# Query-subkey scores from scaled fp16 pairs, with eight smaller moves of work in a two-layer encoder kernel

## The chip, the core and the metric

The kernel is one program on one core of a Trainium2 chip. A core has TensorE (PE in the profile, its weight loads are PEld), VectorE (DVE), ScalarE (ACT), GpSimd (POOL) and SyncE (SP, which here issues nearly all DMAs). Each engine runs its own instruction list in order, and the lists meet only at semaphores. The time is device microseconds of one execution; lower is better.

## The reference, cut to what matters

Two layers run one after the other on x, which is 256 tokens x 1024 channels in float32. Each layer mixes tokens (2-D neighbourhood attention and a long convolution, merged by gates, one output projection, added to x). Then comes the expert retrieval, of which this part matters here:

```python
h = rmsnorm(x, norm2_g[l])
q = (h @ wq).reshape(C, PEER_HEADS, 2, half)             # 8 heads, 2 sides, half = 128
s = jnp.einsum('thpd,hpkd->thpk', q, subkeys)            # 128 subkeys a side
sv, si = lax.top_k(s, PEER_TOPK)                         # 16 best of each side
...
u = u_tab[eid]; a = gelu(einsum('tc,thkc->thk', h, u))   # 128 x 128 experts in all
out = einsum('thk,thkc->tc', g * a, v_tab[eid])
```

## The kernel before, in words

**Weights come as a stream.** All matrices lie in HBM as tiles of 128x1024 float32. SP loads them one after the other into a ring of 4 slots (`refill`). ACT makes of each a scaled fp16 tile `w_hi` (L545) and, for most, scales the float32 tile in place (L552); then POOL (L494) or DVE (L937) subtracts to get the fp16 rest `w_lo`. Activations are held in the same way as a high and a low fp16 part. A product of two matrices is then three fp16 products: high by high, high by low, low by high. `contract` (L1603 to L1617) is one such tile: 16 matmuls of L1611 and 8 of L1615, 256 columns each.

**Stages of a layer.** Tiles 0 to 39 project the input for attention, convolution and gates, 40 to 47 are the two up-projections, 48 to 55 the output projection (`T_OUT`), 56 to 71 the sixteen query tiles (`T_WQ`), 72 to 199 the expert table `u` (`T_U`), 200 to 327 the table `v`.

**The query stage, around which the prediction turns.** Query tile n (0 to 15, two of them for a head) is accumulated in PSUM bank n % 4, from `raw_hi[2]` and `raw_lo[2]`, the residual rows not yet divided by their root mean square. DVE reads the bank, multiplies by the inverse root mean square and writes float32 queries into SBUF: `scale_queries(w, s)` for tile 4w+s (L1389 to L1401), which signals `q2_ready`. PE starts tile n only when `q2_ready` says that tile n-4 has left the bank (L1993). In the same lists, DVE and ACT also make the normalised rows for the expert stage: `make_h` (L998) writes a pair of rows to PSUM, ACT's `norm_high` (L648) copies the pair as fp16, `h_low` (L1006) subtracts. `normalised(2, between)` (L1010) writes out this order by hand and calls `between(s)` at four places in it; with s it scales query tile 4+s. ACT's list for tiles 4 to 7 is: split the next ring tile (`split_behind`, L545 and L552, which waits until PE has finished the tile four before), then `norm_high`.

**Scores.** `subk` holds the layer's subkeys in float32, loaded by a DMA of 1 MB that ACT issues (L817). 32 matmuls a layer of 128x128 by 128 columns, native float32, make the scores in banks 4 to 7 (L2004). ACT copies each bank out (L832, `score_copied`), and DVE searches the top 16 (L1408 on). The first four groups of scores wait for 4, 8, 12 and 16 queries, the last four for a copied bank.

**The rest of the order that the change touches.** `layer_loads` (L398) is SP's list of small loads between the ring's refills. `MASK_AFTER` (L77) says behind which weight tile POOL adds the attention mask to which head's bias. The start of a layer's DVE list (L1092 to L1107), ACT's list around the first normalisation (L685 to L714), around the first softmax heads (L763 to L787), in the up-projection (L800) and in the output projection (L811 to L815), and PE's list between attention and the up-projection (L1900 to L1902) are all written out by hand.

## Time and profile before

| | us |
|---|---|
| median of 3 runs | 1885.17 (1878.71 to 1885.3) |
| the profiled execution's own time | 1882.93 |
| its span, first to last instruction | 1880.9 |
| PE busy | 1861.9 (99%) |
| ACT busy | 1320.0 (70%) |
| DVE busy | 1198.5 (64%) |
| POOL busy | 965.4 (51%) |
| DMA queue of the ring and tables | 58.5% of 16 engines |

The shares are means over the stages. A matmul's end is modelled, so its recorded time (273 ns for 256 columns) is longer than the distance to the next one (about 109 ns) and a short wait of PE can hide in it. The granted clock of TensorE is 1.0 at 2.4 GHz and 0.5 at 1.2 GHz; its mean is 0.998.

### The profile page before, as it was taken

The page shows a single profiled execution, that of the slowest core. Times are in us where ns is not written, and L with a number is a line of the kernel's source. Part 1 is how long each engine was busy: PE and PEld are TensorE (multiplying, and loading weights), DVE is VectorE, ACT ScalarE, POOL GpSimd, SP SyncE. Part 2 cuts the span into 40 slices and gives each one's busy share as a digit, 9 for nine tenths or more (in the row PEclk, how much of TensorE's full clock was granted, in tenths as well). Part 3 has the DMA queues.
Part 4 walks back from the last instruction along what each step waited for, and adds up shares of the span by engine and source line. Part 5 has one row for each costly group of instructions (what it writes and reads, how often), then busy time and mean ns, then how long its engine had stood idle before and what let it go on. Part 6 is the DMA issues. An engine that isn't in the chain of part 4 may idle for free.

```text
span 1880.9 us, 42913 instructions
## 1 busy us (share of the span) xinstructions
PE 1861.9 (99%) x14238; PEld 1352.6 (72%) x14238; DVE 1198.5 (64%) x2529; ACT 1320.0 (70%) x1885; POOL 965.4 (51%) x636
## 2 busy tenths in 40 slices
PE   9899999999999999999999999999999999999999
PEld 7788898899999444444467888988999984444444
DVE  7857489677776444444487573996777764444444
ACT  7877988887777555555578788889877765555554
POOL 1746868876666222222217468687767752222221
PEclk9999999999999999999999999999999999999999
DMA  8644656564555666666575446565555556666664
GB/s 286 177 151 148 228 169 201 201 191 167 167 178 175 204 202 202 203 203 205 191 234 178 157 155 225 169 201 190 191 178 168 168 187 202 203 202 203 204 203 136
DMA packets 100325, 357.39 MB, mean 190 GB/s; under 512 B 11744, under 2 KB 13730, under 8 KB 99492
## 3 DMA queue, kind: packets, MB, share of 16 engines
q1 hardware_dynamic: 99828, 354.36, 58.5%
q10 hardware_dynamic: 432, 2.18, 0.3%
q8 instruction: 39, 0.64, 0.1%
q14 instruction: 26, 0.21, 0.0%
HBM read 355.45 MB, written 1.05 MB: 190 GB/s over the span
## 4 chain that ended last, share of the span: by engine, by line
PE 89%; DVE 4%; ACT 4%; DMA 1%; issue 1%; SPq 0%; ACTq 0%; DVEq 0%
PE bank L2085 35%; PE bank L1611 31%; PE bank L1615 15%; PE bank L2024 3%; ACT w_hi L545 1%; ACT ring L552 1%; DMA ring<-stream 1%; PE bank L2004 1%; DVE w_lo L937 1%; PE bank L1827 0%; ACT raw_hi L604 0%; PE bank L1910 0%; PE bank L1859 0%; DVE bank L998 0%; DMA xT<-x_in 0%
## 5 line engine op out<-in xcount | busy, mean ns | idle before, releaser
L494 POOL TENSOR_TENSOR w_lo<-ring,w_hi 128x1024 f16<-128x1024 f32 x360 | 770.6, 2142 | 413.1 <-ACT ring L552 412.8
L545 ACT ACTIVATE w_hi<-ring 128x1024 f16<-128x1024 f32 x654 | 684.4, 1047 | 33.4 <-PE bank L1597 13.1
L1611 PE MATMUL bank<-act_parts,w_hi 128*128 128x256 f16 x4992 | 597.8, 273 | 0.1
L937 DVE SCALAR_TENSOR_TENSOR w_lo<-ring,w_hi 128x1024 f16<-128x1024 f32 x294 | 361.2, 1229 | 349.0 <-ACT w_hi L545 348.9
L1611 PEld LDWEIGHTS bank<-act_parts,w_hi 128*128 128x128 f16 x4992 | 486.0, 98 | 64.2 <-issue 5.9
L517 POOL TENSOR_TENSOR e_lo<-arena,e_hi 128x256 f16<-128x256 f16 x256 | 174.5, 683 | 482.6 <-ACT e_hi L851 482.6
L2085 PE MATMUL bank<-w_hi,e_hi 128*128 128x512 f16 x1024 | 388.1, 379 | 0.0
L2085 PE MATMUL bank<-w_lo,e_hi 128*128 128x512 f16 x1024 | 388.1, 379 | 0.0
L2085 PE MATMUL bank<-w_hi,e_lo 128*128 128x512 f16 x1024 | 388.1, 379 | 0.0
L552 ACT ACTIVATE ring<-ring 128x1024 f32<-128x1024 f32 x360 | 377.3, 1048 | 0.0
L1615 PE MATMUL bank<-act_parts,w_lo 128*128 128x256 f16 x2496 | 324.2, 273 | 0.0
L851 ACT ACTIVATE e_hi<-arena 128x256 f16 (+1 forms) x256 | 105.9, 416 | 304.8 <-PE bank L2085 304.8
L1615 PEld LDWEIGHTS bank<-act_parts,w_lo 128*128 128x128 f16 x2496 | 244.6, 98 | 28.8
L2085 PEld LDWEIGHTS bank<-w_hi,e_lo 128*128 128x128 f16 x1024 | 100.2, 98 | 120.8
L2085 PEld LDWEIGHTS bank<-w_lo,e_hi 128*128 128x128 f16 x1024 | 100.2, 98 | 120.4
L2085 PEld LDWEIGHTS bank<-w_hi,e_hi 128*128 128x128 f16 x1024 | 100.2, 98 | 120.4
L860 ACT ACTIVATE bank<-bank 128x256 f32<-128x256 f32 x136 | 50.0, 368 | 108.4 <-PE bank L1615 102.3
L1527 DVE SCALAR_TENSOR_TENSOR arena<-arena,bank 128x512 f32 (+1 forms) x128 | 79.4, 682 | 70.8 <-PE bank L2024 70.8
L1516 DVE TENSOR_TENSOR weighted_j<-onehot_j,bank 128x512 f16<-128x512 f16 x256 | 94.8, 411 | 0.0
L1535 DVE TENSOR_TENSOR arena<-arena,bank 128x256 f32 (+1 forms) x136 | 56.8, 418 | 34.1 <-ACT bank L860 24.4
L1611 PE MATMUL bank<-raw_hi,w_hi 128*128 128x256 f16 x336 | 75.6, 273 | 0.8 <-DVE xT L1107 0.8
L1611 PE MATMUL bank<-raw_lo,w_hi 128*128 128x256 f16 x336 | 75.6, 273 | 0.0
(265 smaller groups left out, 1679.8 us busy)
## 6 DMA issues: line engine op xcount, KB each, us to landing
ring<-stream SPq DMA_DIRECT2D x654, 512.0 KB, 4.1
arena<-rpb_in SPq DMA_DIRECT2D x8, 512.0 KB, 8.0
arena<-subkeys ACTq DMA_DIRECT2D x2, 1024.0 KB, 7.7
ring<-stream SPq DMA_DIRECT2D x4, 256.0 KB, 5.0
xT<-x_in SPq DMA_DIRECT2D x4, 256.0 KB, 5.1
arena<-w_in SPq DMA_DIRECT2D x2, 512.0 KB
arena<-decay_in SPq DMA_DIRECT2D x2, 512.0 KB
arena<-dft_in SPq DMA_DIRECT2D x2, 512.0 KB, 5.2
```

Source lines behind the costliest of these rows:

```text
L494: pool.tensor_tensor(w_lo[:, slot, :], ring[:, slot, :], w_hi[:, slot, :], ALU.subtract).then_inc(low_by_pool.sem, 1)
L517: pool.tensor_tensor(e_lo[:, n % RING, :], experts[:, bass.ds(i * RING + n, 1), :].rearrange("p a t -> p (a t)"), e_hi[:, n % RING, :], AL ...
L545: nc.scalar.activation(w_hi[:, slot, :], ring[:, slot, :], ACT.Copy, scale=TABLE_SCALE).then_inc(hi_ready.sem, 1)
L552: nc.scalar.activation(ring[:, slot, :], ring[:, slot, :], ACT.Copy, scale=TABLE_SCALE).then_inc(ring_scaled.sem, 1)
L851: nc.scalar.activation(e_hi[:, n % RING, :], experts[:, bass.ds(i * RING + n, 1), :].rearrange("p a t -> p (a t)"), ACT.Copy).then_inc(e_h ...
L937: V.scalar_tensor_tensor(w_lo[:, slot, :], ring[:, slot, :], TABLE_SCALE, w_hi[:, slot, :], ALU.mult, ALU.subtract).then_inc(low_by_vector ...
L1516: ins = V.tensor_tensor(weighted_j[:, n % BURST, a, :, :, :], onehot_j[:, a, :, :].unsqueeze(1).to_broadcast(wide), pair_weights(a).unsque ...
L1527: V.scalar_tensor_tensor(w, w, EXPERT_SCALE / WEIGHT_SCALE, bank[ROUTE_BANKS[n]][:, :].rearrange("p (t j) -> p j t", t=TOK), ALU.mult, ALU ...
L1535: V.tensor_tensor(w, w, source[n % 2], ALU.mult).then_inc(late_stored.sem, 1)
L1611: T.matmul(out_, weights(w_hi, tile, k), moving[:, k, :], start=(k == 0 and moving is hi), stop=False, skip_group_check=True)
L1615: ins = T.matmul(out_, weights(w_lo, tile, k), hi[:, k, :], start=False, stop=(k == KT - 1), skip_group_check=True)
L2085: ins = T.matmul(bank[4 + 2 * half + tt][:, :], e_[:, slot, tokens], w_[:, slot, columns], start=first and w_ is w_hi and e_ is e_hi, stop ...
```

## The change

The queries are no longer kept in float32. DVE scales the bank in place (`q2_scaled`), ACT copies it as fp16 (`query_high`, `q2_hi_ready`), and DVE subtracts (`query_low`), which is now what signals `q2_ready`. The subkeys are split once a layer, by one ACT and one DVE instruction of 128x2048. The scores become three fp16 products each. Beside that, work is moved: SP's small loads come later and the transform table `dft` in two halves; POOL's mask additions come later; ACT's `norm_high` of the first normalisation comes one tile later each; the first heads' exponentials and normalisation come ahead of a convolution step and a weight split; the second half of the mixed spectrum and its copy come earlier; the last attention part comes later; at the end of the output projection two weight splits come behind the last rows; at the start of the second layer a weight split and a copy change places.

```diff
-MASK_AFTER = (16, 17, 19, 21, 25, 27, 29, 31)
+MASK_AFTER = (21, 22, 23, 25, 27, 29, 31, 33)
...
-        q2T = part(24, 2 * PH, S)
+        q2_hi, q2_lo = halves("q2_hi", 24, 2 * PH), halves("q2_lo", 32, 2 * PH)
+        sub_hi, sub_lo = (halves(name, kb)[:, :, :].rearrange("p k (a n) -> p (k a) n", a=2)
+                          for name, kb in (("sub_hi", 48), ("sub_lo", 52)))
...
                 for slot in range(RING):
                     refill(l, 0, 1, slot)
-                    taps(slot)
                 for slot in range(RING):
                     refill(l, 0, 2, slot)
                     if slot == 0:
-                        small(table_in, dft, dft_in)
+                        small(taps_in, spread, spread_in)
                     elif slot == 2:
-                        small(tables_in, mask, mask_in)
...
+                for slot in range(RING):
+                    refill(l, 0, 3, slot)
+                    if slot == 1:
+                        small(taps_in, skip[0:1, :], skip_in[at, :])
+                        small(taps_in, decay[:, :, :], decay_in)
+                    elif slot == 3:
+                        small(table_in, dft[:, 0:2, :, :], dft_in[:, 0:2, :, :])
...
-                    if 4 <= m <= 6:
-                        norm_high(1, ((0,), (1, 2), (3,))[m - 4])
+                    if m >= 5:
+                        norm_high(1, (m - 5,))
...
+                head_exp(0)
                 hyena_in(10)
-                head_exp(0)
+                head_exp(1)
                 hyena_in(11)
-                head_exp(1)
...
                     raw_high(2, m, bank[4 + m % 4][:, 0:S])
                     square_one(m)
-                    split_behind(T_OUT + m)
+                    if m < KT - 2:
+                        split_behind(T_OUT + m)
+                split_behind(T_OUT + KT - 2)
+                split_behind(T_OUT + KT - 1)
...
+                def query_high(n):
+                    act.wait_ge(q2_scaled.sem, q2_scaled.at(l, n + 1))
+                    nc.scalar.activation(q2_hi[:, n, :], bank[n % 4][:, 0:S], ACT.Copy).then_inc(q2_hi_ready.sem, 1)
                 for s in range(RING):
                     split_behind(T_WQ + s)
                 for s in range(RING):
+                    query_high(s)
                     split_behind(T_WQ + RING + s)
                     norm_high(2, (s,))
-                for tile in range(T_WQ + 3 * RING, T_U + RING):
-                    high_part(l, 0, tile)
-                    scale_tile(tile)
+                for n in range(RING, 2 * PH):
+                    query_high(n)
+                    if n == RING:
+                        act.wait_ge(subk_in.sem, subk_in.at(l, 16))
+                        nc.scalar.activation(sub_hi, subk[:, :, :], ACT.Copy, scale=TABLE_SCALE
+                                             ).then_inc(sub_hi_ready.sem, 1)
+                    if n >= 2 * RING:
+                        high_part(l, 0, T_WQ + RING + n)
+                        scale_tile(T_WQ + RING + n)
...
                 def scale_queries(w, s):
                     dve.wait_ge(tile_done.sem, tile_done.at(l, w * RING + (T_WQ + s + 1)))
-                    V.tensor_tensor(q2T[:, bass.ds(w * RING + s, 1), :].rearrange("p a t -> p (a t)"),
-                                    bank[s % 4][:, 0:S], norm_tmp[:, 2, :], ALU.mult).then_inc(q2_ready.sem, 1)
+                    V.scalar_tensor_tensor(bank[s % 4][:, 0:S], bank[s % 4][:, 0:S], 1.0 / TABLE_SCALE,
+                                           norm_tmp[:, 2, :], ALU.mult, ALU.mult).then_inc(q2_scaled.sem, 1)
+                def query_low(w, s):
+                    dve.wait_ge(q2_hi_ready.sem, q2_hi_ready.at(l, w * RING + s + 1))
+                    n = bass.ds(w * RING + s, 1)
+                    V.tensor_tensor(q2_lo[:, n, :].rearrange("p a t -> p (a t)"), bank[s % 4][:, 0:S],
+                                    q2_hi[:, n, :].rearrange("p a t -> p (a t)"), ALU.subtract
+                                    ).then_inc(q2_ready.sem, 1)
                 for s in range(RING):
                     scale_queries(0, s)
                 dve.wait_ge(out_used.sem, out_used.at(l, 8))
-                normalised(2, lambda s: scale_queries(1, s))
-                with dve.Fori(2, (T_U - T_WQ) // RING) as w:
+                def second_queries(s):
+                    query_low(0, s)
+                    scale_queries(1, s)
+                normalised(2, second_queries)
+                dve.wait_ge(sub_hi_ready.sem, sub_hi_ready.at(l, 1))
+                V.scalar_tensor_tensor(sub_lo, subk[:, :, :], TABLE_SCALE, sub_hi, ALU.mult, ALU.subtract
+                                       ).then_inc(sub_ready.sem, 1)
+                with dve.Fori(1, (T_U - T_WQ) // RING - 1) as w:
                     for s in range(RING):
-                        scale_queries(w, s)
+                        query_low(w, s)
+                        scale_queries(w + 1, s)
+                for s in range(RING):
+                    query_low(3, s)
...
-                pe.wait_ge(subk_in.sem, subk_in.at(l, 16))
+                pe.wait_ge(sub_ready.sem, sub_ready.at(l, 1))
...
-                        ins = T.matmul(bank[4 + g][:, c * P:(c + 1) * P], q2T[:, m, tt * P:(tt + 1) * P],
-                                       subk[:, m, :], start=True, stop=True)
+                        tokens, rows = slice(tt * P, (tt + 1) * P), bank[4 + g][:, c * P:(c + 1) * P]
+                        T.matmul(rows, q2_hi[:, m, tokens], sub_hi[:, m, :], start=True, stop=False)
+                        T.matmul(rows, q2_hi[:, m, tokens], sub_lo[:, m, :], start=False, stop=False)
+                        ins = T.matmul(rows, q2_lo[:, m, tokens], sub_hi[:, m, :], start=False, stop=True)
```

PE's condition for query tile n is the same line as before, `pe.wait_ge(q2_ready.sem, q2_ready.at(l, w * RING + (s - 3)))`; what counts up `q2_ready` is another instruction now.

DVE's list of the kernel before, in each layer from the first normalised rows of the query stage (L998 is `make_h`, L1392 scales a query tile, L1006 is `h_low`):

```order
L998 SCALAR_TENSOR_TENSOR bank<-xT,cols_sb,bank 128x256 [waits out_used]
L998 SCALAR_TENSOR_TENSOR bank<-xT,cols_sb,bank 128x256 x3
L1392 TENSOR_TENSOR arena<-bank,norm_tmp 128x256 [waits tile_done]
L1006 TENSOR_TENSOR act_parts<-bank,act_parts 128x512 [waits h_hi_ready]
L998 SCALAR_TENSOR_TENSOR bank<-xT,cols_sb,bank 128x256 [waits h_ready]
L998 SCALAR_TENSOR_TENSOR bank<-xT,cols_sb,bank 128x256
L1392 TENSOR_TENSOR arena<-bank,norm_tmp 128x256 [waits tile_done]
```

The same stretch of DVE's list in the changed kernel (L1026 is `make_h`, L1430 `query_low`, L1423 the scaling, L1034 `h_low`):

```order
L1026 SCALAR_TENSOR_TENSOR bank<-xT,cols_sb,bank 128x256 [waits out_used]
L1026 SCALAR_TENSOR_TENSOR bank<-xT,cols_sb,bank 128x256 x3
L1430 TENSOR_TENSOR q_lo<-bank,q_hi 128x256 [waits q2_hi_ready]
L1423 SCALAR_TENSOR_TENSOR bank<-bank,norm_tmp 128x256 [waits tile_done]
L1034 TENSOR_TENSOR act_parts<-bank,act_parts 128x512 [waits h_hi_ready]
L1026 SCALAR_TENSOR_TENSOR bank<-xT,cols_sb,bank 128x256 [waits h_ready]
L1026 SCALAR_TENSOR_TENSOR bank<-xT,cols_sb,bank 128x256
L1430 TENSOR_TENSOR q_lo<-bank,q_hi 128x256 [waits q2_hi_ready]
L1423 SCALAR_TENSOR_TENSOR bank<-bank,norm_tmp 128x256 [waits tile_done]
```

The subtraction for query tile 0 now stands behind all four `make_h` instructions, and the one for tile 1 behind the scaling of tile 4, `h_low` and two more `make_h` instructions.

ACT's list of the changed kernel in the same stage, from the fourth split of the stage to the split of the subkeys (L553 and L560 are a ring tile's split, L840 is `query_high`, L656 `norm_high`, L852 `sub_hi`; of the four rounds of L840, L553, L560, L656 the list has between them, the first and the beginning of the next stand here as one run):

```order
L553 ACTIVATE w_hi<-ring 128x1024 [waits tile_done,ring_full3]
L560 ACTIVATE ring<-ring 128x1024
L840 ACTIVATE q_hi<-bank 128x256 [waits q2_scaled]
L553 ACTIVATE w_hi<-ring 128x1024 [waits tile_done,ring_full0]
L560 ACTIVATE ring<-ring 128x1024
L656 ACTIVATE act_parts<-bank 128x512 [waits h_made]
L840 ACTIVATE q_hi<-bank 128x256 [waits q2_scaled]
```

In the kernel before this list reads the same without L840, so the first query's fp16 copy now stands behind four whole splits.

## Rows read from the trace of the kernel before

**Rows 1.** Busy time of each engine (the page).
```profile
PE 1861.9 (99%) x14238; PEld 1352.6 (72%) x14238; DVE 1198.5 (64%) x2529; ACT 1320.0 (70%) x1885; POOL 965.4 (51%) x636
```

**Rows 2.** Waits of PE: line waited for, us in total, times, longest.
```profile
PE bank L1787 <- ACT arena L707: 3.5, 1, 3.5
PE bank L1976 <- DVE raw_lo L971: 2.5, 2, 1.2
PE bank L1859 <- DVE arena L1215: 2.4, 2, 1.2
PE bank L1910 <- DVE arena L1290: 1.5, 2, 0.7
PE bank L1611 <- DVE xT L1107: 0.8, 1, 0.8
```

**Rows 3.** The chain in order of time: start, us, what; scores, routing.
```profile
238.27 7.15 PE bank L2004 x64
...
408.51 1.84 PE bank L2024 x32
```

**Rows 4.** ACT in order of time, end of output projection: start, us, instruction.
```profile
194.09 0.40 ACT L635 ACTIVATE bank<-bank 128x256 f32<-128x256 f32 x1
...
207.89 1.04 ACT L552 ACTIVATE ring<-ring 128x1024 f32<-128x1024 f32 x1
```

**Rows 5.** DVE in order of time, the same stretch and on to query tile 4.
```profile
195.58 0.43 DVE L1379 SCALAR_TENSOR_TENSOR bank<-bank,xT 128x256 f32<-128x256 f32 x1
...
206.87 0.42 DVE L1392 TENSOR_TENSOR arena<-bank,norm_tmp 128x256 f32<-128x256 f32 x1 [1.27 <-PE bank L1615]
207.21 1.66 DVE L998 SCALAR_TENSOR_TENSOR bank<-xT,cols_sb,bank 128x256 f32<-128x256 f32 x4
```

**Rows 6.** PE in order of time, last rows of query tile 4, first of 5.
```profile
208.41 1.04 PE L1615 MATMUL bank<-raw_hi,w_lo 128*128 128x256 f16 x8
209.29 0.27 PE L1611 MATMUL bank<-raw_hi,w_hi 128*128 128x256 f16 x1
```

**Rows 7.** ACT in order of time behind query tile 4.
```profile
209.55 1.06 ACT L545 ACTIVATE w_hi<-ring 128x1024 f16<-128x1024 f32 x1 [0.62 <-PE bank L1615]
...
211.46 0.58 ACT L648 ACTIVATE act_parts<-bank 128x512 f16<-128x512 f32 x1
```

**Rows 8.** DVE in order of time behind query tile 4, and scaling query 9.
```profile
212.07 0.69 DVE L1006 TENSOR_TENSOR act_parts<-bank,act_parts 128x512 f16<-128x512 f32 x1 [2.16 <-ACT act_parts L648]
212.79 0.88 DVE L998 SCALAR_TENSOR_TENSOR bank<-xT,cols_sb,bank 128x256 f32<-128x256 f32 x2
213.58 0.42 DVE L1392 TENSOR_TENSOR arena<-bank,norm_tmp 128x256 f32<-128x256 f32 x1
...
222.73 0.42 DVE L1392 TENSOR_TENSOR arena<-bank,norm_tmp 128x256 f32 x1 [1.78 <-PE bank L1615]
```

**Rows 9.** Groups by line: busy us, mean ns of one.
```profile
L545 ACT ACTIVATE w_hi<-ring 128x1024 f16<-128x1024 f32 x654 | 684.4, 1047 | 33.4 <-PE bank L1597 13.1 <-PE bank L1615 8.6 <-DMA ring<-stream 8.0
L937 DVE SCALAR_TENSOR_TENSOR w_lo<-ring,w_hi 128x1024 f16<-128x1024 f32 x294 | 361.2, 1229 | 349.0 <-ACT w_hi L545 348.9
```

**Rows 10.** Windows: from:to, length, busy us of PE, PEld, DVE, ACT, POOL, PEclk, DMA share, GB/s.
```profile
50.00:52.00 2.00, 0.33 (x4) 0.32 (x4) 2.00 (x2) 1.99 (x3) 2.00 (x1) 0.59 0.99 246
52.00:54.00 2.00, 2.00 (x13) 1.22 (x10) 1.93 (x5) 2.00 (x5) 0.11 (x1) 0.50 1.11 317
...
58.00:60.00 2.00, 2.00 (x26) 1.52 (x19) 1.44 (x3) 2.00 (x4) 0.47 (x1) 1.00 0.87 270
...
190.00:200.00 10.00, 8.61 (x75) 7.15 (x73) 4.76 (x13) 9.98 (x15) 8.33 (x5) 1.00 0.71 247
```

**Rows 11.** The chain: a tile's 16 high matmuls there and later; the table's load.
```profile
39.69 8.20 DMA ring<-stream
...
52.37 3.53 PE bank L1611 x16
...
261.13 1.75 PE bank L1611 x16
```

More of the change, by code:

```diff
@@ L431, in layer_loads @@
                     if slot == 0:
-                        small(table_in, dft, dft_in)
+                        small(taps_in, spread, spread_in)
                     elif slot == 2:
-                        small(tables_in, mask, mask_in)
-                for r in range(ROWS):
-                    for slot in (2 * (r % 2), 2 * (r % 2) + 1):
-                        refill(l, 0, 3 + r // 2, slot)
-                        if slot % 2 == 0:
-                            offsets(r)
-                for group in range(5, T_UP // RING + 1):
+                        small(taps_in, w3, w3_in[at].rearrange("a p b n -> (a p) b n"))
+                for slot in range(RING):
[5 more added lines that the diff above has]
+                        small(table_in, dft[:, 0:2, :, :], dft_in[:, 0:2, :, :])
+                for group in (4, 5):
                     for slot in range(RING):
                         refill(l, 0, group, slot)
+                        if slot % 2:
+                            offsets(2 * (group - 4) + slot // 2)
+                        elif group == 4 and slot == 0:
+                            small(tables_in, mask, mask_in)
+                for group in range(6, T_UP // RING + 1):
+                    for slot in range(RING):
+                        refill(l, 0, group, slot)
+                        if group == 7 and slot == 0:
+                            small(back_in, dft[:, 2:4, :, :], dft_in[:, 2:4, :, :])
                 with sp.Fori(0, (T_VT - T_UP) // RING) as i:
@@ L710, in act_layer @@
                 split_behind(T_V)
+                norm_high(1, (3,))
                 split_behind(T_V + 1)
@@ L739, in act_layer, with gate @@
                     hyena_in(n)
-                def gate(m):
+                def gate(m, between=None):
                     tile_wait(T_GATE + m)
@@ L745, in gate @@
                                          bias=half_gate_b[:, l, m:m + 1]).then_inc(tile_copied.sem, 1)
+                    if between is not None:
+                        between()
                     split_behind(T_GATE + m)
@@ L776, in act_layer @@
                         head_exp(h + 1)
-                    gate(2 * h + 1)
+                    gate(2 * h + 1, (lambda: keep_even(1)) if h == NH - 1 else None)
                     if h % 2 and h + 2 < NH:
@@ L800, in act_layer @@
                 for n in range(T_UP, T_OUT - 1):
+                    if n == T_UP + 4:
+                        merged_high(0)
+                        merged_high(1)
                     split_behind(n)
@@ L1095, in dve_layer @@
                             add_delta(b, delta[b][:, :])
+                    if l and b0:
+                        low_part(l, 0, HEAD)
                     for b in (b0, b0 + 1):
@@ L1105, in dve_layer @@
                         low_part(l, 0, HEAD + b // 2)
-                    if l:
-                        V.tensor_copy(x_pair(b), delta[b][:, :]).then_inc(x_kept.sem, 1)
+                    elif l and b == 0:
+                        low_part(l, 0, HEAD + 1)
                 dve.wait_ge(sq_used.sem, sq_used.at(l, KT // 2))
@@ L1295, in dve_layer @@
                 real_products(1)
-                attention_parts(NH // 2 - 1)
                 def up_product(m):
@@ L1881, in pe_layer, with up @@
                         turn_mixed()
-                def up(n, wait=None):
+                def up(n):
                     for j in (0, 1):
@@ L1892, in up @@
                         for k in range(4):
-                            if wait is not None:
-                                wait(k)
                             first, parts = (0, (attn_hi, attn_lo)) if n < 4 else (4, (act_hi, act_lo))
@@ L1898, in up @@
                         ins.then_inc((up_half, tile_done)[j].sem, 1)
-                mixed_spectrum(1, 0)
-                mixed_spectrum(1, 1)
-                up(0, lambda k: pe.wait_ge(attn_ready.sem, attn_ready.at(l, k + 1)))
+                pe.wait_ge(tile_copied.sem, tile_copied.at(l, 36))
+                parts_ready(0, T_UP)
+                for ks in (range(3), (3,)):
+                    for j in (0, 1):
+                        for k in ks:
+                            pe.wait_ge(attn_ready.sem, attn_ready.at(l, k + 1))
+                            ins = product(bank[j][:, 0:S], T_UP, 4 * j + k, k, k == 0, k == 3, (attn_hi, attn_lo))
+                        if k == 3:
+                            ins.then_inc((up_half, tile_done)[j].sem, 1)
                 up(1)
```

34 lines of the change are left out of this document (18 added, 16 removed).

## The prediction

> **What bounds the kernel now.** I read the busy line first: PE is busy 99% of the span, 1861.9 us, no other engine more than 70% [rows 1]. So an edit counts if it changes PE's work or makes PE wait; the other engines' time is free until PE waits for it. Next the waits of PE [rows 2]: 3.5 us once for the sine of the filter network, then pairs of 1.2, 1.2 and 0.7, one per layer, and 0.8 at the second layer's start. These five rows are 10.7 us, smaller ones some 3 more, so there is little to win by reordering, and much to lose. Third the chain, for what the scores cost: one layer's 32 float32 products stand as 64 matmul records in 7.15 us [rows 3]. Last, the query stage on all three engines, for that is where the change puts new steps between PE and the bank that it wants.
>
> **A tile and its end.** A query tile is 24 matmuls and takes 2.62 us (16 of them 1.75 [rows 11], the other 8 start 0.88 before the next tile [rows 6]). I call T the moment at which PE would start the next tile; for query tile 4 it is 209.29 [rows 6]. ACT's next split, waiting for that tile's end, starts at T+0.26 [rows 7]; a DVE scaling that waits for tile 9 starts at 222.73, where T is 222.39 (209.29 and five tiles), so at T+0.34 [rows 8].
>
> **The scores.** The changed kernel has 96 fp16 matmuls a layer, 128 columns each. The nearest row has the same shape and type: 32 of them in 1.84 us, 57.4 ns each [rows 3], hence 5.5 us against 7.15. ACT's copies are behind them, though: ACT has the last query's copy (0.4) and a split (1.9) ahead of the first bank copy, so the fifth group of scores waits about 0.8. The gain is 1.65 - 0.8, about 0.8 a layer, 1.6 in all. The Trainium skill speaks against the rows here: "TensorE: Matmul & The Clock Gate", section on the back-to-back issue gap, gives about 81 ns for a matmul of 128 columns in a stream with weight loads. By it 96 of them would be 7.8 us, an estimate from that page, and the scores 0.6 us a layer slower than float32; the sum would be some 4.6 us higher. The routing rows, which load weights for every matmul too, show 57.4, so I go by them.
>
> **The query stage, step by step.** `q2_ready` is what lets PE reuse a bank. Before, one DVE instruction behind the tile's end gave it, 3 tiles ahead of need. Now it comes from `query_low`, and that stands in DVE's list behind work that itself waits for later tiles.
>
> Tile 4 wants the low part of query 0. Its fp16 copy stands in ACT's list behind the root and four splits. Before, the last of these ends at 208.93 [rows 4]. The two splits moved behind the output rows don't delay those rows, but ACT idles for the last of them: its square ends at 194.49 [rows 4] and DVE makes the last row at 195.58+0.43 [rows 5], so root and splits come 1.6 later and end at 210.5. Copy 0.4 and subtraction 0.4 give 211.3. PE would be ready at 206.67, or 0.2 earlier, since the last row saves PE that much of its 1.2 wait. The stall is 4.8. Without the 1.6 it would be 3.1; DVE's own list alone (206.87, then 207.21+1.66 [rows 5], then 0.4) would still give 2.6.
>
> Tile 5 wants the low part of query 1. Ahead of it on DVE stands `h_low`, which waits for ACT's `norm_high`, which stands behind a split that waits for tile 4. The trace has this run: split at T+0.26, `norm_high` at T+2.17 to T+2.75 [rows 7], `h_low` at T+2.78, two `make_h` at T+3.50, and free at T+4.29 [rows 8]. Plus 0.42 for the subtraction (the scaling's duration; same operands and size) and 0.06 to PE: 4.8. Before, nobody waited for this run. Tile 6 has the same run behind tile 5: 4.8. Tile 7 has it without `make_h`: 3.9.
>
> Tile 8 wants the low part of query 4, behind the last `h_low` and the subkeys' split. ACT: `norm_high` done as above, one copy to T+3.0, then `sub_hi`, 2048 elements. From 1047 ns for 1024 and 0.58 for 512 I get 2.0 [rows 7, 9]: T+5.0. DVE: `sub_lo` twice the 1229 ns of 1024 less its fixed part, 2.25 [rows 9]: T+7.3. Then the loop's entry and the subtraction: T+7.8. All of it is a stall: 7.8.
>
> Tiles 9 to 15: `query_low(w, s+1)` stands behind `scale_queries(w+1, s)`, which waits for the tile that PE has just finished. So each tile starts after T+0.34, 0.36 for the scaling, 0.45 for the subtraction, 0.06: 1.2 each, 8.4 for seven.
>
> Sum per layer: 4.8 + 4.8 + 4.8 + 3.9 + 7.8 + 8.4 = 34.5, twice 69.0. As bounds I take 57 (3.1 for tile 4, 6.5 for tile 8, 0.9 for each of the seven) and 75 (1.6 for each of the seven, since registers and separate wait instructions lie between them, which no row shows).
>
> **What the stalls do to TensorE's clock.** The trace has one idle of 3.5 us, ahead of the sine's product at 51.7 [rows 2]. The granted clock is 0.59 on the mean from 50 to 52, 0.5 (1.2 GHz) from 52 to 54 and back at 1.0 from 58 [rows 10]. The 16 high matmuls right behind it take 3.53 us instead of 1.75 [rows 11], so a tile at the low level costs 2.6 more. Five stalls a layer are longer than that idle (4.8, 4.8, 4.8, 3.9, 7.8), so I charge the tile behind each: 5 x 2.6 = 13 a layer, 26 in all. From below it is 0 (the clock holds); from above the stage never gets back, as short stalls go on to its end: 12 tiles x 2.6 and 5.5 of scores, 37 a layer.
>
> **The other moves.** The idle of 3.5 ends with a chain through a ring tile that took 8.2 us to land [rows 11]; the change puts about 0.5 MB less of tables in front of it and 1.1 MB later still. If that idle goes, so does its half clock, about 2.9: 6.4 together, of which I take 5. The pairs of 1.2 (softmax against a convolution step), 0.7 (spectrum) and the 0.8 of layer two [rows 2] each have their edit, 4.6 together; I take 4. Nothing new waits there: what moves back has its consumer later in PE's list. So -9, with 0 and -12 as ends. ACT and POOL gain time in the stalls, which PE's later tiles don't need: they are behind PE nowhere else in [rows 2].
>
> **The sum**, against the profiled execution's own 1882.9 (2.0 above its span, 2.2 below the median 1885.2): 1882.9 + 69.0 + 26 - 1.6 - 9 = 1967.3. I predict 1967.
>
> **Rivals.**
> The clock holds, or falls only in the longest stall. For it: the wait of 1.2 before the last output row's products left it at 1.0 [rows 10]. Against it: [rows 10]. The time is 1882.9 + 69 - 1.6 - 9 = 1941, with one fall a layer 1947.
> The clock stays at the low level through tiles 9 to 15 and the scores. For it: those tiles go in bursts with stalls of 1.2. Against it: at [rows 10] it was back within some 6 us of steady work. The time is 1941 + 74 = 2015, with half of the seven 1990.
> Not slower: the new signal comes in time. This would need the subtractions to run before PE asks, so that scores and moves alone are left: 1882.9 - 3.3 - 9 = 1871. It decides at a mean stall of 12.3/24, 0.5 us for each of the 24 tiles from 4 on. Against it stands the order of DVE's list, which makes at least T+0.34 plus two instructions unavoidable for every tile from 9, and [rows 7, 8] for 5 to 7.
> The reordered loads and lists miss their aim (the sine still waits, as its tile is still gated by the same subtraction): 1967 + 9 = 1976. For it: a ring tile is only reloaded after its low part. It lies inside the range.
>
> **How the numbers follow.** Forecast as summed 0.60, clock holds 0.17, clock stays low 0.13, moves without gain 0.07, not slower 0.03. The likeliest case's own range is 1950 to 1985. The range that should hold 8 in 10 reaches down to 1938, to take in the held clock with fewer us of stall, and up to 2000. A measurement of this kernel can't tell less than 0.5%, 9.4 us, from no change; all cases but one lie far above 1895. So slower 0.97, same 0.01, faster 0.02.
>
> **What would show it.** PE waits for the DVE line of `query_low`, some 12 a layer, together near 34 us; at tiles 4 to 8 single idles of 4 to 8 us, the longest behind `sub_lo`; idles near 1.2 from there. A granted clock of 0.5 between about 211 and 250 us in layer one, and the same in layer two. Scores at 57 ns a matmul. The sine's wait below 2 us. It is wrong if PE's waits in the query stage stay below 10 us a layer, or if the stage from the last output tile to the scores' end grows by less than 30 us.

## The result and the profile after

The changed kernel takes 1970.45 us (median of 3 runs, 1968.0 to 1971.21) against 1885.17 before: a ratio of 1.0462, 95% interval 1.0442 to 1.0482. The forecast was 1967. Its profiled execution has a span of 1968.4 us against 1880.9, so 87.5 us are to be placed.

The busy line of the page, against [rows 1]:

```profile
PE 1883.8 (96%) x14302; PEld 1358.2 (69%) x14302; DVE 1223.8 (62%) x2563; ACT 1332.0 (68%) x1919; POOL 969.6 (49%) x636
```

PE has 22 us more of busy time (its matmuls at the low clock count as longer) and 66 us more of idle time; its mean granted clock is 0.982 (before 0.998). The waits of PE (line waited for, us in total, times, longest), against [rows 2]:

```profile
PE bank L1662 <- DVE q_lo L1430: 64.0, 24, 7.4
PE bank L1878 <- DVE arena L1229: 3.3, 2, 3.2
PE bank L1910 <- DVE arena L1246: 2.7, 2, 2.0
PE bank L1644 <- DVE act_parts L1353: 2.3, 2, 1.1
PE bank L2035 <- DVE raw_lo L999: 2.0, 2, 1.0
PE bank L2064 <- ACT arena L860: 1.3, 2, 0.6
...
PE bank L1838 <- ACT arena L715: 0.4, 1, 0.4
```

One row is new and holds nearly everything: 24 waits for the subtraction of `query_low`, twelve a layer, as forecast. The sine's 3.5 is down to 0.4 (last row), but 3.3 at L1878 and 2.3 at L1644 are where 0.5 or less stood. They come back below.

Where the stage lies in the span, PE in order of time: the mean-square product that opens the query stage, and the first product of the expert table behind the scores. Before:

```profile
198.27 0.70 PE L1647 MATMUL bank<-norm_tmp,mats 128*128 128x256 f32 x2 [0.15 <-DVE norm_tmp L982]
...
245.25 0.93 PE L1611 MATMUL bank<-act_parts,w_hi 128*128 128x256 f16 x7
```

After, with the first matmul of query tiles 4 to 10 and the last three scores between them (the bracket is PE's idle time just before, and what ended it):

```profile
196.49 0.70 PE L1698 MATMUL bank<-norm_tmp,mats 128*128 128x256 f32 x2 [0.15 <-DVE norm_tmp L1010]
...
210.34 0.39 PE L1662 MATMUL bank<-raw_hi,w_hi 128*128 128x256 f16 x1 [5.29 <-DVE q_lo L1430]
220.29 0.39 PE L1662 MATMUL bank<-raw_hi,w_hi 128*128 128x256 f16 x1 [4.68 <-DVE q_lo L1430]
230.27 0.39 PE L1662 MATMUL bank<-raw_hi,w_hi 128*128 128x256 f16 x1 [4.68 <-DVE q_lo L1430]
239.34 0.39 PE L1662 MATMUL bank<-raw_hi,w_hi 128*128 128x256 f16 x1 [3.77 <-DVE q_lo L1430]
251.23 0.39 PE L1662 MATMUL bank<-raw_hi,w_hi 128*128 128x256 f16 x1 [7.45 <-DVE q_lo L1430]
257.45 0.28 PE L1662 MATMUL bank<-raw_hi,w_hi 128*128 128x256 f16 x1 [0.92 <-DVE q_lo L1430]
261.17 0.28 PE L1662 MATMUL bank<-raw_hi,w_hi 128*128 128x256 f16 x1 [0.92 <-DVE q_lo L1430]
...
288.56 0.22 PE L2064 MATMUL bank<-sub_hi,q_hi 128*128 128x128 f16 x1
288.62 0.22 PE L2065 MATMUL bank<-sub_lo,q_hi 128*128 128x128 f16 x1
288.67 0.22 PE L2066 MATMUL bank<-sub_hi,q_lo 128*128 128x128 f16 x1
288.73 1.91 PE L1662 MATMUL bank<-act_parts,w_hi 128*128 128x256 f16 x16
```

The stretch grows from 46.98 to 92.24 us in layer 1, and from 46.98 to 89.53 in layer 2: 87.8 of the 87.5 us. Everything else in the kernel sums to about nothing. I use this stretch as the yardstick below, because nearly all the waits that vary with the loads lie outside it.

Two numbers come out of these rows. From 257.45 to 261.17 are 3.72 us, 1.10 more than a tile's 2.62, where the record says 0.92 of idle: about 0.17 of each wait hides behind the last matmul's modelled end. And the distance between starts, less the next idle, is what a tile took: tile 4 took 220.29 - 4.68 - 210.34 = 5.27, tile 9 took 2.80. So tiles 4 to 8 of layer 1 cost 2.5, 2.5, 2.5, 1.7 and 2.5 more than at the full clock, in layer 2 1.6, 2.2, 2.5, 1.4 and 2.4. The windows beside them (columns as in [rows 10]):

```profile
208.00:210.00 2.00, 0.00 (x0) 0.00 (x0) 0.23 (x1) 1.74 (x3) 2.00 (x2) 0.66 0.40 107
210.00:212.00 2.00, 1.66 (x8) 1.19 (x9) 0.20 (x1) 0.00 (x0) 2.00 (x1) 0.50 0.77 242
212.00:214.00 2.00, 2.00 (x12) 1.42 (x10) 0.00 (x0) 0.00 (x0) 0.06 (x1) 0.50 0.84 283
...
216.00:218.00 2.00, 0.00 (x0) 0.00 (x0) 0.08 (x1) 2.00 (x3) 0.21 (x1) 1.00 0.00 0
218.00:220.00 2.00, 0.00 (x0) 0.00 (x0) 1.74 (x4) 0.47 (x2) 1.91 (x1) 0.72 0.00 0
```

The granted clock (the third number from the right, 1.00 until 208) falls while PE stands idle, from 208 to 210, is 0.5 over tile 4, is back at 1.0 when PE stands idle again at 216, and falls anew before 220. Part of the low level thus lies over time in which PE does nothing, and costs nothing there.

The stall of tile 8 in full, against [rows 7, 8] (ACT, then DVE):

```profile
243.88 1.06 ACT L553 ACTIVATE w_hi<-ring 128x1024 f16<-128x1024 f32 x1 [5.45 <-PE bank L1666]
244.84 1.04 ACT L560 ACTIVATE ring<-ring 128x1024 f32<-128x1024 f32 x1
245.79 0.58 ACT L656 ACTIVATE act_parts<-bank 128x512 f16<-128x512 f32 x1
246.27 0.37 ACT L840 ACTIVATE q_hi<-bank 128x256 f16<-128x256 f32 x1
246.53 1.91 ACT L852 ACTIVATE sub_hi<-arena 128x2048 f16<-128x2048 f32 x1
```
```profile
243.82 0.43 DVE L1423 SCALAR_TENSOR_TENSOR bank<-bank,norm_tmp 128x256 f32<-128x256 f32 x1 [4.62 <-PE bank L1666]
246.40 0.69 DVE L1034 TENSOR_TENSOR act_parts<-bank,act_parts 128x512 f16<-128x512 f32 x1 [2.14 <-ACT act_parts L656]
248.47 2.29 DVE L1445 SCALAR_TENSOR_TENSOR sub_lo<-arena,sub_hi 128x2048 f16<-128x2048 f32 x1 [1.38 <-ACT sub_hi L852]
250.68 0.42 DVE L1430 TENSOR_TENSOR q_lo<-bank,q_hi 128x256 f32 x1
```

PE's tile ends near 243.7. Then one step follows another: ACT's split of a ring tile, its copies of the rows and of a query, `sub_hi`, and on DVE `sub_lo` and the subtraction. PE starts at 251.23. `sub_lo` takes 2.29 where 2.25 was worked out, `sub_hi` 1.91 for 2.0.

### The profile page after: what moved, and what is told of

Read it like the earlier page. It is cut to its first block, busy times and chain, and to the rows that moved or that the text cites. A ratio compares the mean times of both kernels' runs of the same rounds, so it can differ in the third digit from the quotient of the medians.

```text
span 1968.4 us, 43125 instructions
## 1 busy us (share of the span) xinstructions
PE 1883.8 (96%) x14302; PEld 1358.2 (69%) x14302; DVE 1223.8 (62%) x2563; ACT 1332.0 (68%) x1919; POOL 969.6 (49%) x636
## 4 chain that ended last, share of the span: by engine, by line
PE 82%; DVE 6%; ACT 6%; DMA 3%; issue 2%; POOL 1%; SPq 0%; DVEq 0%; ACTq 0%
PE bank L2146 34%; PE bank L1662 28%; PE bank L1666 14%; PE bank L2085 3%; DMA ring<-stream 2%; ACT w_hi L553 2%; ACT ring L560 2%; DVE w_lo L965 1%; POOL w_lo L502 1%; DVE bank L1026 1%; DVE q_lo L1430 0%; DMA arena<-rpb_in 0%; DVE arena L1246 0%; PE bank L1992 0%; PE bank L1969 0%
## 5 line engine op out<-in xcount | busy, mean ns | idle before, releaser
L553 ACT ACTIVATE w_hi<-ring 128x1024 f16<-128x1024 f32 x654 | 684.3, 1047 | 78.3 <-PE bank L1666 50.1
L965 DVE SCALAR_TENSOR_TENSOR w_lo<-ring,w_hi 128x1024 f16<-128x1024 f32 x294 | 372.0, 1265 | 348.6 <-ACT w_hi L553 348.5
L560 ACT ACTIVATE ring<-ring 128x1024 f32<-128x1024 f32 x360 | 377.1, 1048 | 0.0
L1662 PE MATMUL bank<-raw_hi,w_hi 128*128 128x256 f16 x336 | 91.0, 307 | 64.0 <-DVE q_lo L1430 64.0
L1662 PEld LDWEIGHTS bank<-raw_hi,w_hi 128*128 128x128 f16 x336 | 36.7, 109 | 78.8 <-issue 71.6
L1662 PE MATMUL bank<-raw_lo,w_hi 128*128 128x256 f16 x336 | 90.9, 307 | 0.0
```

Source lines behind the costliest of these rows:

```text
L553: nc.scalar.activation(w_hi[:, slot, :], ring[:, slot, :], ACT.Copy, scale=TABLE_SCALE).then_inc(hi_ready.sem, 1)
L560: nc.scalar.activation(ring[:, slot, :], ring[:, slot, :], ACT.Copy, scale=TABLE_SCALE).then_inc(ring_scaled.sem, 1)
L965: V.scalar_tensor_tensor(w_lo[:, slot, :], ring[:, slot, :], TABLE_SCALE, w_hi[:, slot, :], ALU.mult, ALU.subtract).then_inc(low_by_vector ...
L1662: T.matmul(out_, weights(w_hi, tile, k), moving[:, k, :], start=(k == 0 and moving is hi), stop=False, skip_group_check=True)
```

## The experiments

All were run beside the kernel before; its median was 1883.12 in the first set, 1881.3 in the second, 1882.23 in the third, so ratios are compared, not times. The diffs show the lines of an edit on which it turns, not the whole edit.

**The parts apart.** The first kernel has the moves alone: the changed kernel with the old queries, the old scores and `scale_queries` alone in `normalised`.

```diff
-                    query_low(0, s)
                     scale_queries(1, s)
```

> All the moves of the change, with float32 queries and scores as before. Theory: the whole loss is in the query stage. The changed kernel's trace starts the query stage's second tile 1.8 us earlier in layer one and then, from there to the same place of layer two, runs 1.3 us longer apart from the stage itself, so the moves are worth about nothing: 1885, ratio 0.998 to 1.002. Rival, the term of the prediction: the moves give 9 us, 1876, ratio 0.995.

Measured: 1884.25 us, ratio 1.0005 (0.9992 to 1.0019). The second has the pairs alone, in the kernel before:

```diff
                 for s in range(RING):
+                    query_high(s)
                     split_behind(T_WQ + RING + s)
```

> The kernel before with the fp16 pairs alone, no moves. Theory: 1971, ratio near 1.046, with the same five long and seven short waits of PE a layer. Rival: the moves of work help elsewhere by 9 us, then 1980. A second rival, that the moved splits of the output projection cause tile 4's wait: then its wait falls from 5.3 and 4.3 to about 3.1.

Measured: 1961.79 us, ratio 1.0418 (1.04 to 1.0435), and a query stage of 88.96 and 86.98 us. So the pairs are the slowdown, and the moves, for which I had booked 9 us of gain, bring none. But the pairs alone came 9 us lower than my theory had them (7 us by the ratios, 1.0462 against 1.0418): pairs and moves together are dearer than their sum. Of this kernel, the start of tiles 4 and 5 in layer 2:

```profile
1182.43 0.28 PE L1649 MATMUL bank<-raw_hi,w_hi 128*128 128x256 f16 x1 [3.15 <-DVE q_lo L1417]
1189.90 0.39 PE L1649 MATMUL bank<-raw_hi,w_hi 128*128 128x256 f16 x1 [4.68 <-DVE q_lo L1417]
```

Tile 4 waits 3.15 (2.97 in layer 1) instead of 4.3 to 5.3, and in layer 2 it then runs at full clock: 1189.90 - 4.68 - 1182.43 = 2.79. In layer 1, after 2.97, it took 4.46.

**The link between them.** Pairs, and of the moves only the two weight splits behind the last output rows:

```diff
-                    split_behind(T_OUT + m)
+                    if m < KT - 2:
+                        split_behind(T_OUT + m)
+                split_behind(T_OUT + KT - 2)
+                split_behind(T_OUT + KT - 1)
```

> The kernel before with the pairs and with one of the moves, the two weight splits of the output projection put behind the last rows. Theory A (this move is what makes the pairs dearer beside the moves): the first query's fp16 copy comes some 1.6 us later, tile 4's wait grows to 5.3 and 4.3 us in the two layers, and the clock falls at tile 4 in both layers, 1.7 to 2.6 us each; 2 x (1.6 + 1.7 to 2.6) less the last row's 0.4 gives 6 to 8 us over the 1961.8 of the pairs alone, 1968 to 1970. Theory B (the addition comes from elsewhere: the two later moves, or another clock pattern): no more than 2 us over the pairs alone, 1962 to 1964.

Measured: 1965.88 us, ratio 1.045 (1.0427 to 1.0473). Tile 4 now waits 4.32 in both layers and runs at the low clock in both; the query stage is 89.73 and 89.76, so 0.8 and 2.8 longer than with the pairs alone. The time lies between the two theories, and its interval overlaps that of the pairs alone; the rows of tile 4 decide. Theory A holds in kind, at about two thirds of its size in layer 2 and less in layer 1, where the clock had already fallen. The mechanism shows on ACT: it has nothing to do until DVE delivers the last output row, and the split that would have filled the time stands behind it (this is the same row as in the changed kernel, 194.51 there):

```profile
196.70 0.47 ACT L610 ACTIVATE raw_hi<-bank,cols_sb 128x256 f16<-128x256 f32 x1 [1.55 <-DVE bank L1400]
```

The changed kernel's tile 4 in layer 1 waits another 0.97, since one of its splits found its ring tile not landed:

```profile
203.69 1.06 ACT L553 ACTIVATE w_hi<-ring 128x1024 f16<-128x1024 f32 x1 [0.86 <-DMA ring<-stream]
```

**The clock.** The changed kernel with matmuls that only keep PE busy while it would wait, their results going to an unused bank; nothing is left out:

```diff
+                fill = {4: 17, 5: 19, 6: 19, 7: 15, 8: 31}
+                for n in range(RING, 2 * PH):
+                    for _ in range(fill.get(n, 0)):
+                        T.matmul(bank[5][:, 0:P], w_rest[:, :], w_rest[:, :], start=True, stop=True)
```

> The changed kernel, with zero float32 products of 128x128 by 128 columns into an unused bank put ahead of PE's waits for query tiles 4 to 8 (17, 19, 19, 15 and 31 of them, each about 0.22 us and together less than the wait, so that PE is busy in most of it); PE's loop over these tiles is written out. It splits wait from clock. Theory: the waits end at the same distance from the tile before, the granted clock stays at 1.0 and tiles 4 to 8 take 2.6 us: by the tile times in the trace that gives back 11.7 us in layer one and 10.0 in layer two, 1949. Rival: the slow tiles are part of the waiting (weights that come late) and not the clock: then 1970.

Measured: 1947.19 us, ratio 1.0349 (1.0329 to 1.0368). The windows of the stage are at 1.00 throughout, where the changed kernel has 0.67 or 0.68 in each ten us from 210 to 260:

```profile
210.00:220.00 10.00, 9.64 (x88) 9.13 (x87) 2.76 (x6) 4.52 (x6) 2.13 (x1) 1.00 0.39 133
...
230.00:240.00 10.00, 9.55 (x87) 9.11 (x86) 3.75 (x4) 5.38 (x8) 2.13 (x1) 1.00 0.33 105
```

The query stage is 79.70 and 78.75 us, 12.5 and 10.8 less than in the changed kernel, 23.3 in all. Not all of that is the clock. The steps of tiles 9 to 15, which were at 1.00 in both kernels and have no filling, are 3.64 instead of 3.71, and the stalls of tiles 4 to 8 are shorter by as much: 24 x 0.07 = 1.7. PE's loop over the tiles is written out in this kernel, which is the likely reason, but that was not tried by itself. What the clock took is the rest, 21.6. The waits themselves stayed nearly as long, only filled: tiles 4 and 5 start 7.40 us apart, 2.62 of tile and 4.78 of stall, where the changed kernel has 4.68 + 0.17.

**Single stalls.** Only the split of the subkeys comes three tiles later, on ACT as shown, and on DVE behind the subtraction of query 6:

```diff
-                    if n == RING:
+                    if n == RING + 3:
                         act.wait_ge(subk_in.sem, subk_in.at(l, 16))
```

> The changed kernel with one thing moved: the split of the subkeys (one ACT and one DVE instruction, 128x2048) stands three tiles later, behind the copy and the subtraction of queries 7 and 6. Theory A (tile 8's wait of 7.4 us is the run of work before it plus the split's 3.6): tile 8 waits 3.8 us, the same 3.6 us appear again as a wait only as far as the split still stands ahead of a later subtraction (tile 10 or 11 waits 2 to 4.5 instead of 0.9), time 1970 - 0 to 7, so 1963 to 1970. Theory B (the split is worth what it delays tile 8 by, and costs nothing later): 1963 or less, and no wait over 1.5 us behind tile 8.

Measured: 1961.21 us, ratio 1.042 (1.04 to 1.0441), 0.0042 or 7.9 us below the changed kernel (the two query stages are 8.2 shorter). Tile 8 waits 3.77, like tile 7, and the next waits are short:

```profile
245.35 0.39 PE L1663 MATMUL bank<-raw_hi,w_hi 128*128 128x256 f16 x1 [3.77 <-DVE q_lo L1430]
251.58 0.28 PE L1663 MATMUL bank<-raw_hi,w_hi 128*128 128x256 f16 x1 [0.93 <-DVE q_lo L1430]
```

Theory B is right: the split is worth 2 x 3.68 and comes back nowhere. Three tiles later it stands in the time in which DVE waits for PE's next tile anyway: DVE's idle time before the next scaling falls from 2.96 to 0.34.

In the next kernel the order is changed for tiles 9 to 15 alone. The subtractions of queries 5 to 7 no longer stand behind a scaling, and those of the later queries stand behind the scaling of the next query, not of the third one after:

```diff
-                with dve.Fori(1, (T_U - T_WQ) // RING - 1) as w:
+                for s in range(RING):
+                    query_low(1, s)
+                for w in (2, 3):
                     for s in range(RING):
-                        query_low(w, s)
-                        scale_queries(w + 1, s)
-                for s in range(RING):
-                    query_low(3, s)
+                        scale_queries(w, s)
+                        if w == 3 or s:
+                            query_low(w, s - 1) if s else query_low(w - 1, 3)
+                query_low(3, 3)
```

> The changed kernel with the order changed for tiles 9 to 15 alone: there the subtraction of a query stands one tile later than the scaling that frees it, so that the scaling of the tile just finished is no longer ahead of the subtraction that PE waits for. Theory A (each of these waits is only the scaling and the subtraction behind the tile's end, nothing else): the fourteen waits of about 0.9 in the records vanish, tiles 4 to 8 wait as before, 14 x 1.09 = 15.3 us less, 1955. Theory B (the copies on ACT, which stand behind its splits, take the DVE order's place as what is late): half of it or less, 1962 to 1970.

Measured: 1955.64 us, ratio 1.0389 (1.0366 to 1.0411). Its waits of PE:

```profile
PE bank L1664 <- DVE q_lo L1430: 51.8, 10, 7.5
```

Ten waits instead of 24: all fourteen short ones are gone. 0.0073 of 1882 is 13.7 us of the 15.3 expected, the rest within the intervals; the two query stages are 16.1 shorter. Theory A.

**The order turned round.** The changed kernel with every subtraction one tile behind the scaling, and the first copies between the splits on ACT:

```diff
-                    query_low(0, s)
+                    query_low(0, 3) if s == 0 else query_low(1, s - 1)
                     scale_queries(1, s)
```

> The changed kernel with another order alone: ACT copies a query's high part right behind the split that the tile's end allows (the first three behind the second split), and DVE subtracts one tile later than it scales, with the subkeys' split behind the second of the last eight tiles. Theory: tile n's low part is ready about 3 us behind its end, PE wants the bank 7.9 us behind it, so no waits are left: 1970 - 68 of waits - 22 of clock = 1880 to 1882, ratio 0.996 to 0.998. Rival: ACT, now with 0.36 a query and 1.9 for the subkeys more, falls behind PE's 2.62 us a tile and the ring's splits come late: then waits on the high parts and 1890 or more.

Measured: 1885.99 us, ratio 1.0016 (1.0004 to 1.0029), above the 1880 to 1882 of my theory. The order was the whole slowdown but for some 4 us (the stages are 48.87 and 48.80), since two waits stood where I had expected none, 2.8 in all at tile 4 and 3.8 at the scores:

```profile
PE bank L1885 <- DVE arena L1233: 4.4, 2, 2.3
PE bank L2071 <- DVE q_lo L1433: 3.8, 2, 2.0
PE bank L1669 <- DVE q_lo L1433: 2.8, 2, 1.6
```

The last query's copy stands on ACT behind a split, and the subtraction behind it. So the same order went into the kernel before, with no move at all, and that split was put behind the fourth copy of the scores (the diff is against the order just described):

```diff
                 for n in range(2 * RING, 2 * PH):
-                    high_part(l, 0, T_WQ + RING + n)
-                    scale_tile(T_WQ + RING + n)
+                    if n < 2 * PH - 1:
+                        high_part(l, 0, T_WQ + RING + n)
+                        scale_tile(T_WQ + RING + n)
                     query_high(n)
...
+                    if n == 3:
+                        high_part(l, 0, T_U + RING - 1)
+                        scale_tile(T_U + RING - 1)
```

> The kernel before with the pairs alone, the subtractions put one tile behind the scaling on DVE, the fp16 copies of the first queries put between ACT's splits, the last query's copy put ahead of the last split, and that split behind the fourth score copy. Theory A (the scores are worth 1.65 us a layer, and nothing of them is lost once no copy is late): no wait over 0.3 us for a subtraction, no wait of 2.0 before the last groups of scores; 1883.1 - 3.3 = 1879.8, a ratio of 0.997 to 0.999. Theory B (the copies on ACT and the subtractions on DVE always cost PE something at tile 4 and at the scores): 1883 to 1886, ratio 1.000 to 1.002.

Measured: 1878.52 us, ratio 0.998 (0.9965 to 0.9994): 0.2% below the kernel before, and the interval just leaves out 1. The stage shows it without scatter. In layer 2 the query stage takes 45.19 us, 1.79 less than before, with no wait for a subtraction; in layer 1 one of 1.5 at tile 4 stays, behind a split that waited 2.71 for its ring tile, so theory A holds but for that. The 16-bit products are thus a small gain, in layer 2 of the size that [rows 3] had promised.

**Where the moves' gain went.** The changed kernel once more, with the pairs in the good order, the later loads, masks, `norm_high` and the earlier spectrum kept, and four moves taken back, of which these are two:

```diff
-                    if n == T_UP + 4:
-                        merged_high(0)
-                        merged_high(1)
                     split_behind(n)
...
-                head_exp(0)
                 hyena_in(10)
-                head_exp(1)
+                head_exp(0)
                 hyena_in(11)
+                head_exp(1)
```

What the expectation calls the late last attention part is the first of them: ACT's copies of the first two merged rows, which the changed kernel has ahead of a weight split. DVE's late attention part itself stays.

> The changed kernel with the same order of copies and subtractions as in the kernel just described, with its later loads, its later masks, its later norm_high and its spectrum move kept, and with four moves taken back: the softmax heads' order, the late last attention part, the output projection's splits, and the start of the second layer. Theory A (the kept moves take the sine's idle of 3.5 and its half clock of 2.9, and the waits of the others came from the four that are taken back): 1883.1 - 3.3 - 6.4 - 1.5 = 1872, ratio 0.993 to 0.996. Theory B (the later table loads crowd ring tiles and turn the sine's idle into another wait in the first layer): one wait of 2 to 3.5 us in the first layer before the sine or behind it, 1878 to 1882, ratio 0.997 to 1.000.

Measured: 1878.62 us, ratio 0.999 (0.9977 to 1.0002). The query stage takes 45.19 and 45.20, and the sine's wait is gone, but there are waits of 2.36, 2.00 and 1.70 at two lines of attention:

```profile
PE bank L1912 <- DVE arena L1245: 3.9, 3, 2.0
...
PE bank L1880 <- DVE arena L1228: 2.4, 1, 2.4
```

Theory B in kind, though one of the waits is in layer 2. The same with the loads and masks as before (the edit is that of the last kernel below, in the same places):

> The best combination of the last call with the table loads, the transform table's halves and the masks as in the kernel before; kept are the pairs in the order without waits, the later norm_high of the first normalisation and the earlier spectrum. Theory A (the later loads bring nothing that lasts: they take away the sine's idle and give two waits of 2.0 to 2.4 on the tables): as fast as with them or faster, a ratio of 0.996 to 0.999, the waits of 2.4 and 2.0 gone, the sine's idle back at least in one layer. Theory B (they bring the 6 us forecast): slower than with them, ratio 1.000 to 1.002.

Measured: 1878.97 us, ratio 0.9977 (0.9964 to 0.999), theory A; the wait of 2.36 is gone, those of 2.0 and 1.7 are the 1.2 and 1.2 of [rows 2] again, and the sine's is back, 4.8 in layer 1 of this execution:

```profile
PE bank L1838 <- ACT arena L713: 4.8, 1, 4.8
...
PE bank L1910 <- DVE arena L1243: 2.4, 2, 1.2
```

And the moves alone with the loads and masks as before:

```diff
-MASK_AFTER = (21, 22, 23, 25, 27, 29, 31, 33)
+MASK_AFTER = (16, 17, 19, 21, 25, 27, 29, 31)
```

> The moves without the pairs, and of the moves the table loads, the transform table's halves and the mask additions put back as in the kernel before. Theory A (the later loads take the sine's idle, but cost about as much by a later wait with half clock in the first layer): the sine's idle of 3.5 is back with its half clock, the wait of some 3 us behind it is gone, and the time is that of all the moves together, 1884 within 1.5. Theory B (the loads gain the 6.4 us that I forecast, and the order moves lose as much): 1888 to 1891. Theory C (the loads cost more than they gain): 1879 to 1882.

Measured: 1884.05 us beside 1881.3, ratio 1.0016 (1.0001 to 1.0031), against 1.0005 with the later loads. The sine waits 1.3 and 2.4 us. Of the three, theory A is the nearest: the loads trade one wait for others, and no pair of kernels with and without them can be told apart. The intervals (some 2.5 us each way) leave a gain or loss of 2 us open.

## Why the forecast came near: two sizes off, in opposite directions

Taken step by step against the changed kernel's profile:

- **Order of the subtractions, 69.0 us forecast.** The records give 64.0 in 24 waits, and 24 x 0.17 hidden behind modelled ends: 68.1. By tile in layer 1 (forecast, record + 0.17): 4.8, 5.5; 4.8, 4.85; 4.8, 4.85; 3.9, 3.9; 7.8, 7.6; and 1.2, 1.1 for each of the seven. The reading of [rows 7, 8], a run of dependent instructions that nobody waited for until a new wait was put behind it, is what carried the forecast; the two kernels under Single stalls confirm two of its terms by taking them away. The lower bound of this term was added up wrongly: the terms that the prediction names give 2 x 29.4 = 59, not 57. Nothing hangs on it.
- **Tile 4.** Forecast 3.1 without the 1.6 of ACT's idle time at the last output row, and 4.8 with it. The runs show 3.1 and 3.3 in the pairs alone, 4.5 with the splits moved (0.17 added). The step held, and it is a case of an edit that looks harmless, a split moved behind rows that it would not have delayed, and that costs only because a new consumer stands at the end of the same list.
- **The clock, 26 us forecast.** The tiles cost 11.7 and 9.9, in sum 21.6; the filled kernel, from the other side, gives the same, 23.3 less the 1.7 of shorter steps. The mis-sized term is the flat 2.6 for each tile: a whole tile at 1.2 GHz. The stage has five such stalls a layer, but in tile 7 of both layers, and in tile 4 of layer 2, the level was back at 1.0 before the tile's end. In layer 2, tile 4 runs from 1188.43 to about 1192.8:

```profile
1190.00:1192.00 2.00, 2.00 (x13) 1.47 (x12) 0.00 (x0) 0.00 (x0) 0.36 (x1) 0.58 0.70 244
1192.00:1194.00 2.00, 0.79 (x8) 0.46 (x5) 0.43 (x1) 1.12 (x2) 0.00 (x0) 1.00 0.54 213
```

  The mechanism was right, and neither rival (clock holds 1941, clock stays low 2015) was: behind the waits of 0.92, tiles 9 to 15 ran at 2.8 us and 1.00.
- **The scores, -1.6.** In the changed kernel they follow one another in steps of 57 ns (288.56, 288.62, 288.67, 288.73 in the rows above), so 96 take 5.4 us against 7.15 [rows 3], and the wait for the fifth group is 0.64 + 0.17 for 0.8 forecast. The 81 ns that the Trainium skill gives in "TensorE: Matmul & The Clock Gate", section on the back-to-back issue gap, does not hold for this stream with a weight load for each product.
- **The other moves, -9 forecast, about 0 measured.** This is the step that failed, in the sentence "Nothing new waits there: what moves back has its consumer later in PE's list". The gains came nearly as booked. The sine's wait and its low clock went in the profiled execution (3.5 to 0.4, and 2.9), so did the spectrum's 0.7 a layer, and 0.25 a layer at the last output row; the 0.8 at the second layer's start only changed its line. That is some 8 us. Against them stand 3.3 at L1878, which brought the clock to 0.50 from 80 to 82 us and so cost 1.7 more, 2.0 in layer 2 at L1910, where the softmax heads' move had made 0.65 of 1.2 in layer 1 (and 0.66 and 0.62 in the last kernel above), and 1.15 a layer at L1644 where 0.27 stood: some 7. The wait at L1878 begins on ACT, where a ring tile is late, in the stretch into which the table loads were moved:

```profile
63.50 1.06 ACT L553 ACTIVATE w_hi<-ring 128x1024 f16<-128x1024 f32 x1 [2.27 <-DMA ring<-stream]
...
78.69 1.90 PE L1878 MATMUL bank<-arena 64*128 64x256 f32 x8 [3.16 <-DVE arena L1229]
```

From 40 to 80 us a ring tile took 9.8 us to land (median of 12) against 3.3 before. That the later loads make the wait at L1878 is shown by the two combinations, which differ in loads and masks alone (2.36 against none), and by the rest: the line waits 0.8 to 3.2 us at its longest in all seven kernels with the later loads, and less than 0.3 in all six with the old ones; the wait of 2.0 at the line of L1910 goes with them in the same way. The path from the late ring tile to it was read, not tested. The wait at L1644 is 1.15 in all seven kernels in which ACT copies the first two merged rows ahead of a weight split, and 0.27 in all six without that move; it was not tried by itself.

The rival "miss their aim" had this size, no gain from the moves, with a chance of 0.07, but not this way: the sine's wait did go in the changed kernel, and others came.

Put together: 1882.9 + 68.1 + 21.6 - 1.9 + 0 = 1970.7 against the measured 1970.45. Against that the forecast of 1967.3 was 0.9 too high in the stalls, 4.4 in the clock and 0.3 in the scores, and 9 too low in the moves. With the clock's price alone put right it would have said 1963: that it came within 3.2 us is luck, two errors that met.

## What to carry to other kernels

When an edit changes which instruction signals that a buffer is free, follow the signalling engine's list backwards from it: every instruction ahead of it that waits for a later step of the waiting engine turns into a stall, however idle that engine is on the page. A copy or a subtraction that a later step needs belongs one step behind its input in each list; here it then cost no wait in layer 2 and one of 1.5 us in layer 1. The same instructions in another order made the difference between 4.2% slower and 0.2% faster. And when a wait is removed by loading something later, look at the stretch that now gets the load: here it got waits of its own, of up to 3.2 us.

## What the runs showed of the hardware

- **The same wait does not always lower the clock.** With the pairs alone, tile 4 ran at 1.2 GHz after a wait of 2.97 in layer 1 and at 2.4 GHz after 3.15 in layer 2 (4.46 us for the tile against 2.79). With the moves alone, waits of only 2.0 were followed by the low level in both layers (the windows of layer 1):

```profile
100.00:102.00 2.00, 0.15 (x1) 0.15 (x2) 1.93 (x5) 2.00 (x3) 0.00 (x0) 1.00 0.12 12
102.00:104.00 2.00, 2.00 (x12) 1.51 (x12) 1.93 (x5) 0.84 (x2) 1.68 (x1) 0.56 0.91 320
104.00:106.00 2.00, 2.00 (x13) 1.48 (x12) 1.97 (x2) 0.00 (x0) 2.00 (x2) 0.59 1.00 401
```

  In the best combination, waits of 2.36 and 2.0 left it at 1.00. So a stall of 2 to 3.5 us has a price of its own length or of about 2 us more (1.7 at tile 4, and 1.7 behind the wait at L1878), and a forecast should carry both. What decides between them no run shows.
- **A low clock costs only where PE works.** In the changed kernel it fell between 208 and 210 us and again between 218 and 220, both times with PE idle, and the part of the low level that lay ahead of PE's next tile cost nothing.
